# The PLE gate takes unscaled input and scales its product, and UP2's input lies in front of its hidden tiles

## The reference, cut to what matters

```python
def rms_norm(x, g):
    return x * rsqrt(mean(x * x, axis=-1) + EPS) * g

x = x + (gelu(conv(up[..., :3072])) * up[..., 3072:]) @ w_down      # DN1
g_ple = sigmoid(rms_norm(x, ple_norm) @ w_ple_gate)                 # PG
x = x + g_ple * (p @ w_ple_proj)                                    # PR
gate, up = split(rms_norm(x, ffn1_norm) @ ffn1_w_in)                # UP2
x = x + 0.5 * (silu(gate) * up) @ ffn1_w_out                        # DN2
u = rms_norm(x, mix_norm)                                           # into QA and on
```

## Time and profile before

| | us |
|---|---|
| median of 3 runs | 1086.37 |
| the runs | 1086.37, 1088.42, 1084.81 |
| the profiled execution, its whole time | 1091.5 |
| its span, first to last instruction | 1089.4 |
| PE busy | 1063.6 |
| DVE busy | 760.6 |
| ACT busy | 582.7 |
| POOL busy | 198.6 |

### The profile page before, as it was taken

How to read it: one execution, slowest core, us unless ns; L and a number is a source line. 1 busy time by engine, 2 the same in 40 slices (tenths; PEclk the granted TensorE clock), 3 DMA queues, 4 the chain that set the end, 5 groups by cost and what they waited for, 6 DMA issues and landing times.

```text
span 1089.4 us, 19093 instructions
## 1 busy us (share of the span) xinstructions
PE 1063.6 (98%) x7174; PEld 972.2 (89%) x7174; DVE 760.6 (70%) x885; ACT 582.7 (53%) x805; POOL 198.6 (18%) x224
## 2 busy tenths in 40 slices
PE   7999999999989999999999999999999999999998
PEld 6999999999868887899888888999999998888887
DVE  4478975756878886557788866585665777887554
ACT  4455588635555554347644445455555455444443
POOL 3001101205222221014222231010000142222210
PEclk8999999999989999999999999999999999999999
DMA  7635355664756654675666626764444457665463
GB/s 227 196 105 167 99 176 191 219 205 139 191 147 186 184 153 129 186 239 166 194 192 187 180 85 198 220 213 154 155 155 159 157 150 201 187 190 151 125 194 109
DMA packets 289745, 186.93 MB, mean 172 GB/s; under 512 B 6703, under 2 KB 286326, under 8 KB 289686
## 3 DMA queue, kind: packets, MB, share of 16 engines
q1 hardware_dynamic: 289566, 186.02, 57.4%
q10 hardware_dynamic: 120, 0.09, 0.0%
HBM read 184.94 MB, written 1.08 MB: 171 GB/s over the span
## 4 chain that ended last, share of the span: by engine, by line
PE 81%; DVE 7%; ACT 5%; issue 3%; DMA 2%; POOL 1%; SPq 0%; ACTq 0%; DVEq 0%
PE psum L1697 31%; PE psum L1734 17%; PE psum L1698 16%; PE psum L1690 3%; PE psum L1692 3%; PE psum L1691 3%; DVE wl L1167 2%; ACT wh L537 2%; PE psum L1793 1%; PE psum L1801 1%; PE psum L1794 1%; PE psum L1795 1%; PE psum L1979 1%; PE psum L1760 1%; DMA raw<-in_w_mix_in 1%
## 5 line engine op out<-in xcount | busy, mean ns | idle before, releaser
L1167 DVE TENSOR_TENSOR wl<-raw,wh 128x2048 fp32r<-128x2048 f32 (+3 forms) x211 | 421.4, 2002 | 150.5 <-ACT wh L537 147.9
L1697 PE MATMUL psum<-xx,wh 128*128 128x512 f32 x1072 | 376.2, 395 | 5.3 <-DVE wl L1167 3.4
L537 ACT ACTIVATE wh<-raw 128x2048 fp32r<-128x2048 f32 (+3 forms) x212 | 335.5, 1588 | 69.8 <-PE psum L1692 31.7
L1698 PE MATMUL psum<-xx,wl 128*128 128x256 f32 x1072 | 300.1, 280 | 0.0
L1697 PEld LDWEIGHTS psum<-xx,wh 128*128 128x128 f32 x1072 | 202.0, 188 | 52.0 <-DVE wl L1167 4.0
L1698 PEld LDWEIGHTS psum<-xx,wl 128*128 128x128 f32 x1072 | 203.4, 190 | 0.1
L1697 PE MATMUL psum<-hx,wh 128*128 128x512 f32 x556 | 198.6, 401 | 4.4 <-DVE wl L1167 4.4
L1698 PE MATMUL psum<-hx,wl 128*128 128x256 f32 x556 | 156.7, 282 | 0.0
L1734 PE MATMUL psum<-xx,wh 128*128 128x256 f32 x800 | 148.9, 288 | 1.6 <-DVE wl L1167 1.6
L1697 PEld LDWEIGHTS psum<-hx,wh 128*128 128x128 f32 x556 | 105.2, 189 | 31.1 <-DVE wl L1167 5.6
L1734 PEld LDWEIGHTS psum<-xx,wh 128*128 128x128 f32 x800 | 126.4, 194 | 3.4 <-DVE wl L1167 1.8
(11 more groups left out here) (258 smaller groups left out, 1350.4 us busy)
## 6 DMA issues: line engine op xcount, KB each, us to landing
raw<-in_ffn_w_in SPq DMA_DIRECT2D x88, 512.0 KB
raw<-in_w_in SPq DMA_DIRECT2D x24, 1024.0 KB
raw<-in_w_up SPq DMA_DIRECT2D x48, 512.0 KB
raw<-in_w_mix_in SPq DMA_DIRECT2D x20, 1024.0 KB
raw<-in_ffn_w_out SPq DMA_DIRECT2D x32, 448.0 KB
raw<-in_w_down SPq DMA_DIRECT2D x24, 512.0 KB
raw<-in_ffn_w_out SPq DMA_DIRECT2D x16, 512.0 KB
raw<-in_w_attn_br SPq DMA_DIRECT2D x4, 1024.0 KB
```

The lines of the kernel that those rows point to most:

```text
L537: act.activation(wh[:, u % RING, 0:w], raw[:, u % RING, 0:w], ACT.Copy).then_inc(rounded, 1)
L1167: dve.tensor_tensor(wl[:, s, 0:w], raw[:, s, 0:w], wh[:, s, 0:w].bitcast(F32), ALU.subtract).then_inc(rest, 1)
L1697: mm(ps, w, both.rearrange("p h t -> p (h t)"), start=first, stop=False)
L1698: return mm(ps[:, 0:T], wl[:, slot, w0:w0 + P], both[:, 0, :], start=False, stop=last)
```

## The change

The gate's norm goes from the scaled to the unscaled way. `UNSCALED` gets norm 2 and `WRITTEN` loses it: DN1 now makes the unscaled tiles for it, as DN2 does for norm 4, in `xx`. The gate multiplies them, DVE multiplies the bank by the inverse into `page_x`, and ACT takes the sigmoid in place, SBUF to SBUF. `norm_behind(2, PR)` takes the place of `normalize(2)` and of the two halves of a remainder: unscaled tile 7, the remainder of the gate's first unit, the diagonal, the remainder of the second. On ACT `copy_inv(2)` stands ahead of the projection's evacuations. POOL's `split_norm(2)` is gone. `hx` and `xx` become views of one tensor `parts` of 32 tiles: UP2's and QA's unscaled input lies in its tiles 0 to 7, UP2's hidden tiles in 8 to 29, and norm 4's scaled tiles in `xx` (24 to 31). Indices of semaphores follow. The diff, cut to its core:

```diff
 READER = {n: "A" for n in ("KI", "QI", "K", "V", "Q", "LG0", "LG1", "LG2", "LG3", "RI0", "GA", "RI1", "GB", "PR",
-                           "PG", "KA", "VA", "QB", "KB", "VB", "GA'", "GB'")}
+                           "KA", "VA", "QB", "KB", "VB", "GA'", "GB'")}
...
 for _name, _n in [("N0", POOL_LOWS), ("CONV", 4), ("Y0", 2), ("Y1", 2), ("MRG1", 4), ("N1", POOL_LOWS), ("H1", H1), ("P", 1),
-                  ("N2", POOL_LOWS), ("H2", H2), ("N4", POOL_LOWS), ("MRG2", 4), ("H3", H2)]:
+                  ("H2", H2), ("N4", POOL_LOWS), ("MRG2", 4), ("H3", H2)]:
...
 HI, _at = {}, 0
-for _name, _n in [("N0", K), ("MRG1", 4), ("N1", K), ("N2", K), ("N4", K), ("MRG2", 4)]:
+for _name, _n in [("N0", K), ("MRG1", 4), ("N1", K), ("N4", K), ("MRG2", 4)]:
...
-UNSCALED = {1: 0, 3: 1, 4: 2, 5: 3}
-
-WRITTEN = {0: 0, 1: 1, 2: 2, 4: 3}
+UNSCALED = {1: 0, 2: 1, 3: 2, 4: 3, 5: 4}
+
+WRITTEN = {0: 0, 1: 1, 4: 2}
+
+HIDDEN = {"UP1": 0, "UP2": K, "UP3": 0}
...
-        xx = sb("xx", [P, K, 2, T], F32R)
-        hx = sb("hx", [P, H1, 2, T], F32R)
+        parts = sb("parts", [P, H1 + K, 2, T], F32R)
+        hx, xx = parts[:, 0:H1, :, :], parts[:, H1:H1 + K, :, :]
...
-            return (hh, hl, 16) if n == 1 else (xh, xl, 0)
-
-        def normed(n):
-
-            return (hh, hl, 16) if n in (2, 4) else (xh, xl, 0)
+            return (hh, hl, 16) if n == 1 else (hh, hl, 0) if n in (3, 4) else (xh, xl, 0)
...
                         at = c + i2
-                        out_tile = xh[:, at:at + 1, :] if isinstance(at, int) else xh[:, bass.ds(at, 1), :]
+                        high = unscaled(n)[0]
+                        out_tile = high[:, at:at + 1, :] if isinstance(at, int) else high[:, bass.ds(at, 1), :]
...
-            for m in range(2):
-                evac(group(U["PR"]) + m, page_g[:, 2 * m:2 * m + 2, :])
-            norm_high(2)
-            for m in range(2, 4):
+            copy_inv(2)
+            for m in range(4):
...
                 if m < 3:
-                    evac(group(U["PG"] + m), page_x[:, 2 * m:2 * m + 2, :], func=ACT.Sigmoid)
+                    act.wait_ge(read_d, READ_BY["D"][group(U["PG"] + m) + 1])
+                    part = page_x[:, 2 * m:2 * m + 2, :]
+                    act.activation(part, part, ACT.Sigmoid).then_inc(gate_done, 1)
...
                     unscaled_high(3, 2 * m, 2)
-            g = group(U["PG"] + 3)
-            group_done(g)
-            for s, signal in ((0, gate_half), (1, read_a)):
-                act.activation(page_x[:, 6 + s, :], bank(g)[:, s * T:(s + 1) * T], ACT.Sigmoid).then_inc(signal, 1)
+            for s, (signal, value) in enumerate(((gate_half, 1), (read_d, READ_BY["D"][group(U["PG"] + 3) + 1]))):
+                act.wait_ge(signal, value)
+                act.activation(page_x[:, 6 + s, :], page_x[:, 6 + s, :], ACT.Sigmoid).then_inc(gate_done, 1)
...
                     pool.wait_ge(prod_done, prods + r + 1 + 3 * i)
-                    if j is None:
-                        high, low = hh[:, bass.ds(i * 3 + r, 1), :], hl[:, bass.ds(i * 3 + r, 1), :]
-                    else:
-                        high, low = hh[:, j:j + 1, :], hl[:, j:j + 1, :]
+                    at = bass.ds(i * 3 + r + HIDDEN[name], 1) if j is None else slice(j + HIDDEN[name], j + HIDDEN[name] + 1)
+                    high, low = parts[:, at, 0, :], parts[:, at, 1, :]
...
             split(hh[:, 0:2, :], hl[:, 0:2, :], pT[:, :, :])
-            split_norm(2, "N2")
...
-                if n == 4:
+                if n in (2, 4):
...
                             dve.wait_ge(ux_high, 8 * UNSCALED[n] + s + 1 + c3 * 3)
-                            dve.scalar_tensor_tensor(out=xl[:, at, :], in0=x[:, at, :], scalar=param(NORMS[n], c3 * 3 + s),
-                                                     in1=xh[:, at, :].bitcast(F32), op0=ALU.mult, op1=ALU.subtract).then_inc(ux_low, 1)
+                            high, low, _ = unscaled(n)
+                            dve.scalar_tensor_tensor(out=low[:, at, :], in0=x[:, at, :], scalar=param(NORMS[n], c3 * 3 + s),
+                                                     in1=high[:, at, :].bitcast(F32), op0=ALU.mult, op1=ALU.subtract).then_inc(ux_low, 1)
...
                         unscaled_low(n, 6, 1)
-                if name == "DN1":
-                    rest_half(U[name] + 25, 0, early_half)
...
             mask_bias(2, bias4)
-            ffn_down("DN1", 1.0)
-            normalize(2)
-            rest_half(U["PG"], 1, rest)
-            rest_unit(U["PR"] + 2)
+            ffn_down("DN1", 1.0, 2)
+            norm_behind(2, U["PR"])
+            inv = root[:, T:2 * T]
+            dve.wait_ge(inv_copied, UNSCALED[2] + 1)
...
                 part, pr = page_x[:, 2 * m:2 * m + 2, :], page_g[:, 2 * m:2 * m + 2, :]
+                g = group(U["PG"]) + m
+                dve.wait_ge(mm_done, g + 1)
+                if m < 3:
+                    dve.tensor_tensor(part, bank(g)[:, :].rearrange("p (s t) -> p s t", s=2),
+                                      inv.unsqueeze(1).to_broadcast([P, 2, T]), ALU.mult).then_inc(read_d, 1)
+                else:
+                    for s, signal in ((0, gate_half), (1, read_d)):
+                        dve.tensor_tensor(part[:, s, :], bank(g)[:, s * T:(s + 1) * T], inv, ALU.mult).then_inc(signal, 1)
+                dve.wait_ge(read_a, READ_BY["A"][group(U["PR"]) + m + 1])
                 for n, (a, b) in enumerate(((0, 2),) if m < 3 else ((0, 1), (1, 2))):
-                    if m == 3 and n == 0:
-                        dve.wait_ge(gate_half, 1)
-                    else:
-                        dve.wait_ge(read_a, READ_BY["A"][group(U["PG"] + m) + 1])
+                    dve.wait_ge(gate_done, m + n + 1)
...
                 before = group(U[{1: "WO", 3: "PG", 5: "WO2"}[n]])
-                signal, readers = (read_a, READ_BY["A"]) if n == 3 else (read_d, READ_BY["D"])
                 unit_ready(u)
-                pe.wait_ge(signal, readers[before + (2 if n == 3 else 1)])
+                pe.wait_ge(read_d, READ_BY["D"][before + (2 if n == 3 else 1)])
...
                 spread_inv(n)
-                pe.wait_ge(signal, readers[before + (4 if n == 3 else 3)])
+                pe.wait_ge(read_d, READ_BY["D"][before + (4 if n == 3 else 3)])
...
                 else:
-                    up_first_two(u0, n, xx, 0)
-                    split_pair(u0 + 2, RING_BASE[2])
+                    both = hx if n == 3 else xx
+                    up_first_two(u0, n, both, 0)
+                    split_pair(u0 + 2, RING_BASE[2], 0, both)
...
                         pe.wait_ge(read_d, READ_BY["D"][g0 + begun + r - 2] + 3 * i)
-                        split_pair(u0 + begun + r, RING_BASE[r], i)
+                        split_pair(u0 + begun + r, RING_BASE[r], i, xx if n == 1 else both)
...
                     pe.wait_ge(read_d, READ_BY["D"][g0 + r - 2])
-                    split_pair(u0 + r, RING_BASE[r % 3])
-
-            def ffn_down(name, parts, lows, n):
+                    split_pair(u0 + r, RING_BASE[r % 3], 0, both)
+
+            def ffn_down(name, pieces, lows, n):
...
                 u0, g0 = U[name], group(U[name])
+                hidden = parts[:, HIDDEN["UP" + name[2]]:H1 + K, :, :]
...
                     k0 = 0
-                    for r, nk in enumerate(parts):
+                    for r, nk in enumerate(pieces):
...
                                 pe.wait_ge(lo_done, lows + k0 + k + 1)
-                            first, last = k0 + k == 0, k0 + k == sum(parts) - 1
+                            first, last = k0 + k == 0, k0 + k == sum(pieces) - 1
                             if c == 7:
-                                ins = three(ps[:, 0:T], u % RING, k * P, hh[:, k0 + k, :], hl[:, k0 + k, :], first, last)
+                                ins = three(ps[:, 0:T], u % RING, k * P, hidden[:, k0 + k, 0, :], hidden[:, k0 + k, 1, :], first, last)
                             else:
-                                ins = split_product(ps, u % RING, k * P, hx[:, k0 + k, :, :], first, last)
+                                ins = split_product(ps, u % RING, k * P, hidden[:, k0 + k, :, :], first, last)
...
-            pe.wait_ge(early_half, 1)
-            bank_free(group(U["PG"]))
-            half_pair(U["PG"], 0, (0, 2), lambda k: pe.wait_ge(xh_done, HI["N2"] + k + 1), hh, hl, 16)
-            half_pair(U["PG"], 0, (1,), lambda k: low_ready(2, k), hh, hl, 16)
-            unit_ready(U["PG"])
-            half_pair(U["PG"], 1, high=hh, low=hl, t0=16).then_inc(mm_done, 1)
-            for m in range(1, 4):
-                pair(U["PG"] + m, parts=normed(2))
+            pe.wait_ge(ux_low, 8 * UNSCALED[2] + 8)
+            for m in range(4):
+                pair(U["PG"] + m)
...
                 if e in (4, 5, 10, 11):
-                    tokens(u, normed(4))
+                    tokens(u)
...
                 elif e != 1:
-                    pair(u, parts=normed(4))
```

(16 more changed lines are left out.)

## The result

The changed kernel takes 1091.95 us (median of 22 runs, 1087.91 to 1098.57) where the kernel before, run beside it, takes 1087.51 (22 runs, 1083.67 to 1093.02): 1.0042 times as long, with an interval of 1.0024 to 1.0061. It is slower by about 4.6 us. The forecast was 1088.2 us, 1.85 more than before, and the range ended at 1091.6. Both were put on the 1086.37 that the first three runs of the kernel before had; over 22 runs it has 1087.51. As differences, 4.6 us stand against a forecast of 1.85 and an upper end of 5.2.

What follows compares the result with a forecast made beforehand. PE was taken as the bound: busy 98% of the span, 81% of the chain. Later inverse +0.86, norm chain gone -1.72, DVE behind PE +2.7 gave +1.85 on 1086.37, so 1088.2 us; range -2.0 to +5.2 us.

Steps and rivals of the forecast that it cites:

- Step 1: Ahead of the gate: the norm chain of scaled tiles goes, returning at most 1.72 us to PE.
- step 3: At the gate's start: the inverse comes later, PE waits 0.9 us at its broadcast; 0.86 us in the sum.
- Step 2: In DN1: unscaled tiles are made there, with ACT's copies and DVE's subtractions fitting into 1.9 us of slack; cost nothing.
- (b): Rival: in DN1 ACT's copies delay the roundings and so PE in seven columns; +4.0 us, chance 0.08.
- Steps 4 and 6: Gate's second unit is ready in time, covered by 0.8 us; tile layout, UP2 and loads cost 0.
- (a): Rival: DVE keeps up and PE runs the gate through; -0.5 us, at best -0.9, chance 0.2.
- (c): Rival: the gate's stall was its weights, not the norm, and comes back; +3.6 us, chance 0.03.
- Step 5: In the gate: DVE's multiply and its wait for the sigmoid make a pair 6.69 us against PE's 5.76; +2.7 us.
- The bound above (+3.1): Upper bound in the gate: first pair's subtractions as slow as the others (+0.49), each multiply at 0.93 us (+0.72).

Runs made afterwards that it cites:

- no_scale: Changed kernel without DVE's multiply by the inverse, the sigmoid straight out of PSUM, so another gate is computed; 0.9993 of the kernel before.
- layout_alone: Kernel before with only the new tile layout (one tensor for both sets), its gate still on scaled input; 0.9975 of the kernel before.
- lows_behind: Changed kernel with DVE's low parts of the first two pairs of x tiles moved behind the next unit's multiply; 1.0027 of the kernel before.
- useful_fill: Changed kernel with PE's work at UP2's start reordered, tiles 0 to 5 of both halves ahead of tiles 6 and 7; 0.9993 of the kernel before.
- late23: Kernel before with an unused 2.3 us DVE add ahead of the last gate unit's half products; 1.0036 of the kernel before.
- diag_first: Changed kernel with the gate's diagonal put ahead of the remainder of the gate's first unit; one run of 1095.38 us.
- fill18: Changed kernel with 18 useless 256-column matmuls between UP2's input tiles 5 and 6, where PE waits; 1.0005 of the kernel before.
- all_three: Changed kernel with the edits of useful_fill, lows_behind and diag_first together; 0.9986 of the kernel before, 0.9983 when timed again.
- before_pe_order: Kernel before with only PE's new order of work at UP2's start; 0.9986 of the kernel before.

## Why the prediction was wrong

- **Step 1** (1.72 us back) and **step 3** (0.86 paid): right. Gate at 7.68 against 6.86 is 0.82; both together are no_scale's -0.89.
- **Step 2** (DN1 free): right; no new wait of PE in DN1, and rival (b) fell with it. **Steps 4 and 6**: right; layout_alone for the layout. The 0.25 us that PE waits for the last gate unit was not forecast and costs nothing, as DVE is the bound there. Rivals (a) and (c) fell as well: DVE waits for PE once, and the gate's stall did not come back.
- **Step 5** (DVE becomes the bound): the mechanism was right, the term too small. First multiply at 13.71, 13.68 forecast. Product behind multiply: 1.82 us in the first pair and 1.44 in the others, where I had 1.38; last half 0.96, where I had 0.82. That makes 0.44 + 0.06 + 0.06 + 0.14 = 0.7: 2.57 where I had 1.85. In the first pair the sigmoid runs from 496.79 to 497.42 and the product starts at 497.88; every version with the multiply has these 0.46 us, and what DVE does in them stays open. The slow subtractions (1.84) were priced right, and lows_behind shows that the price hangs on their place: behind the next multiply two of them take 0.87 together. The multiply out of PSUM took 0.67 to 0.69, the same as the product with both inputs in SBUF (0.69). The dearer PSUM source of the Trainium skill, VectorE: DVE Perf Modes, in its TRN2 errata, did not show in these rows.
- **The step that failed** is the end of step 5: "Everything behind hangs on it", and so "**That is 1.85 us later**" for all behind the half product as for the product itself. It took a wait of PE to cost its own length. Behind PE's 2.34 us the clock fell, which costs another 2.3 to 3.1 us. The forecast named the wait for tile 6 and gave it no second price. Measured, 2.57 + 2.8 = 5.4 at the spreading and at DN2's begin (the mean of three), of which 5.0 is left at DN2's last add; the timing has 4.6. The bound above (+3.1) was a bound on DVE alone, and its 2.57 lies inside it.
- **The range** ended 5.2 us above the kernel before, and 4.6 is below that. This is luck: the room above 3.1 was made for DN1 and for noise, and neither is what filled it. The time of 1091.95 lies beyond 1091.6 all the same, since the kernel before has 1087.51 over 22 runs, 1.1 more than the three runs that the sum was put on.

## What to carry to other kernels

A wait of PE can cost twice: its length, and half the speed for some us behind it (here 2.3 to 3.1 us on top of 2.34). Where a change swaps a short wait of PE for a longer one, look at the granted clock behind such waits elsewhere in the same trace, and if it falls there, add that price. It is often cheaper to reorder PE's own work into the wait (useful_fill, 5.6 us at DN2's begin) than to shorten what it waits for (lows_behind, 1.8 us off the chain and the clock lost all the same).

Taking the scale out of a product's input moves work behind the product. If it then sits in a round trip between two engines, put other work of the waiting engine into it.

## What the runs showed of the hardware

- **Whether the clock falls differs between executions of one kernel, and it falls more often at long waits.** Over the 18 profiles, at the start of UP2: behind waits of 2.0 to 2.4 us 6 of 6 fell (changed, late23, lows_behind, diag_first); behind 0.46 and 0.34 us 2 of 7; in the kernels whose wait is filled or reordered 0 of 5, though two of these (fill18, useful_fill) still wait 0.7 us ahead of UP2. At DN2's end PE waits 0.3 to 2.7 us: of the six waits of 1.76 us and more four saw a fall (1.76, 2.04, 2.27, 2.65; not 1.84 and 1.90), of the twelve of up to 1.60 none. Elsewhere: 3.3 to 3.4 us in UP1 15 of 18; 2.1 to 2.2 us in DN1's first column 13 of 18; 1.6 us some 305 us ahead of A 0 of 18; 1.08 us in DN2's and DN3's first columns 0 of 36. A fall lasts 3.4 or 6.8 us at these places. The Trainium skill, TensorE: Matmul & The Clock Gate, in Part 1 on the clock gate, says that the chip sets this clock by how busy PE has lately been, and looks at times that are not tied to the kernel's start. The traces agree: the first half fits the counts by length of the wait, the second no_scale, which lost the clock in two of three profiles at the same waits.
- **Runs differ in the first 34 us.** In the 9 profiles with A at 486 or more POOL's first five subtractions take 6.95 to 7.00 us and let PE wait 2.8 us near 23 us, and the clock is low until 31 to 34; in the 9 with A at 477 to 483 they take 3.7 us and that wait is absent. The changed kernel, no_scale and all_three have both kinds; the kernel before has the late kind in all three profiles, and its variants late23, layout_alone and before_pe_order the early one. Why POOL takes longer stays open. This swing of 5 us and more is larger than the change, so a single profile's span says nothing of it, and marks inside the trace do.
- **PE has two rates in DN2 at a granted clock of 1.00.** Its 344 matmuls from DN2's begin to DN2's end (first start to last start) take 56.1 us in 6 of the 18 profiles and 57.0 in 12, with no wait among them; both rates occur with either gate. The cause stays open.
